# A two-layer RWKV-7 and retention encoder step on one core: full transposes for a pair's states and head factors, branch A's gates left in place, one projection unit moved

## The reference

```python
z = h @ p['w_in']
za, zb, zg = jnp.split(z, [A_COLS, A_COLS + B_COLS], axis=-1)
y_a, new_rwkv = _rwkv7_branch(za_mix, s_rwkv, p)      # 16 heads of 64
y_b, new_ret = _retention_branch(zb, s_ret, pos)      # 4 heads, 256 x 512 states
merged = gates[:, :, 0] * (y_a @ w_branch_a) + gates[:, :, 1] * (y_b @ w_branch_b)
out = merged @ p['w_out']
```

## Time and profile before

| | |
|---|---|
| median of 3 runs | 4438.86 us (4438.25 to 4439.08) |
| the profiled execution | 4447.02 us |
| its span, first to last instruction | 4445.2 us |
| TensorE busy | 4177.0 us, 94% |
| VectorE, ScalarE, GpSimd busy | 44%, 31%, 7% |
| mean granted TensorE clock | 0.964 |
| the eight pairs of layer 0, of layer 1 | 130 to 1188 us, 2360 to 3414 us |
| branch A beside the first head | 1216 to 1327 us, 3441 to 3552 us |

### The profile page before, as it was taken

One profiled execution on the slowest core, in us unless ns is written; L12 is line 12 of the kernel. 1 busy time (PEld: TensorE's weight loads), 2 busy tenths in 40 slices (PEclk: granted clock), 3 DMA queues, 4 the chain that ended last, 5 costly groups with the idle time before them and its releaser, 6 DMA issues.

```text
span 4445.2 us, 86915 instructions
## 1 busy us (share of the span) xinstructions
PE 4177.0 (94%) x37570; PEld 3719.6 (84%) x37570; DVE 1960.5 (44%) x3036; ACT 1389.4 (31%) x2167; POOL 291.5 (7%) x467
## 2 busy tenths in 40 slices
PE   6999999999989988999989999999999899889997
PEld 5888899888866677999978888998888666779997
DVE  3534444434245544333354444444342455454444
ACT  4333333333313223222233233333332132232222
POOL 1000000000011111000100000000000111000000
PEclk8999999999989997999989999999999899989998
DMA  5112212222356564334421122112223565412222
GB/s 186 58 59 66 69 59 62 62 62 70 104 167 207 183 206 150 117 121 125 119 76 59 59 65 68 59 60 64 61 69 109 166 207 181 156 37 74 76 74 69
DMA packets 477367, 448.86 MB, mean 101 GB/s; under 512 B 18894, under 2 KB 409096, under 8 KB 476112
## 3 DMA queue, kind: packets, MB, share of 16 engines
q1 hardware_dynamic: 417712, 253.05, 18.8%
q0 software_dynamic: 41888, 157.01, 10.9%
q10 hardware_dynamic: 17408, 33.56, 2.0%
HBM read 345.79 MB, written 97.76 MB: 100 GB/s over the span
## 4 chain that ended last, share of the span: by engine, by line
PE 85%; DVE 7%; DMA 3%; ACT 3%; issue 2%; POOL 0%; ACTq 0%; DVEq 0%; SPq 0%; POOLq 0%
PE ps L739 83%; DVE scr L1927 2%; PE ps L743 2%; DMA w_raw<-in_w_branch_a_dram 1%; ACT scr L1385 1%; ACT w_hi L1398 1%; DMA scr<-in_ada_w_dram 1%; DVE acc L1927 1%; DVE w_lo L1940 1%; DVE h_lo L1927 1%; DVE lw L1927 1%; DMA w_raw<-in_w_out_dram 1%; DVE scr L1929 0%; ACT scr L1535 0%; DVE acc L2322 0%
## 5 line engine op out<-in xcount | busy, mean ns | idle before, releaser
L739 PE MATMUL ps<-h_hi,w_hi 128*128 128x320 f32 x4544 | 1105.3, 325 | 97.4 <-DVEq L1935 56.1
L739 PE MATMUL ps<-h_lo,w_hi 128*128 128x320 f32 x4544 | 1043.3, 311 | 0.0
L739 PE MATMUL ps<-h_hi,w_lo 128*128 128x320 f32 x4544 | 1041.8, 311 | 0.0
L739 PEld LDWEIGHTS ps<-h_hi,w_hi 128*128 128x128 f32 x4544 | 749.6, 190 | 186.0 <-issue 160.3
L739 PE MATMUL ps<-scr 64*64 64x64 f32 (+10 forms) x13248 | 809.5, 250 | 14.0 <-ACTq L1517 14.0
L739 PEld LDWEIGHTS ps<-scr 64*64 64x64 f32 (+4 forms) x13248 | 590.8, 141 | 212.5 <-issue 182.7
L739 PEld LDWEIGHTS ps<-h_lo,w_hi 128*128 128x128 f32 x4544 | 767.4, 190 | 0.0
L739 PEld LDWEIGHTS ps<-h_hi,w_lo 128*128 128x128 f32 x4544 | 767.0, 190 | 0.0
L1398 ACT ACTIVATE w_hi<-w_raw 128x1024 fp32r<-128x1024 f32 (+1 forms) x468 | 410.7, 878 | 796.5 <-PE ps L739 591.8
L1940 DVE TENSOR_TENSOR w_lo<-w_raw,w_hi 128x1024 fp32r<-128x1024 f32 (+1 forms) x468 | 469.5, 1003 | 366.0 <-ACT w_hi L1398 347.3
L1385 ACT ACTIVATE scr<-ps 128x512 f32<-128x512 f32 (+9 forms) x723 | 343.8, 475 | 759.9 <-PE ps L739 544.4
(11 more groups left out here) (152 smaller groups left out, 2899.7 us busy)
## 6 DMA issues: line engine op xcount, KB each, us to landing
w_raw<-in_w_in_dram SPq DMA_DIRECT2D x180, 512.0 KB, 3.7
scratch_z<-scr SPq DMA_DIRECT2D x128, 320.0 KB, 2.2
scr<-in_ada_w_dram POOLq DMA_DIRECT2D x40, 1024.0 KB, 6.8
scr<-in_state_ret_dram POOLq DMA_DIRECT2D x64, 512.0 KB, 4.9
out_dram<-scr ACTq DMA_DIRECT2D x64, 512.0 KB, 3.0
w_raw<-in_w_ffn_up_dram SPq DMA_DIRECT2D x64, 512.0 KB, 4.0
w_raw<-in_w_ffn_down_dram SPq DMA_DIRECT2D x128, 256.0 KB, 2.7
scr<-scratch_z POOLq DMA_DIRECT2D x24, 1280.0 KB, 9.3
```

Of the source, the lines that this page charges most:

```text
L739: return pe.matmul(out, lhsT, rhs, start=start, stop=stop, skip_group_check=True)
```

## The change

- The sample states of a pair are loaded with the even streams on the first and the odd streams on the last 64 partitions (before: streams 0 to 3 and 4 to 7), so that two streams are turned by one full 128 x 128 transpose: four instead of eight products on the way in (`sT`) and on the way out (`sout`). The stores follow.
- The prompt state is turned in bank 3 instead of bank 4, and the next pair's first scores no longer wait for ScalarE's copy of it; the second block's scores do, with the wait for `sout`.
- `over_channels` becomes five full transposes of factors that VectorE has first widened to 128 x 640 (`widen`), in `yb` for the keys and in `t1` for the group norm.
- The first inverse level: only one of the two orientations of each block is copied through TensorE; the other is multiplied with its mask straight from `LTI` by VectorE, 64 partitions at a time, after the z products.
- `POINTS`: one unit behind the u/w products instead of two, two behind `cb3` instead of one.
- Branch A: the last two gates of a layer are not stored, they stay in `ZT`; the tiles are done in the order 6, 7, 0, ..., 5, so that these two serve first. POOL's two loads go. SyncE's queue issues the weight of a tile first, and then the gate of the tile before.

```diff
@@ -107,6 +107,7 @@
 SPILLED = Z_ALL + 16
+STORED = SPILLED - 2
...
@@ -115,7 +116,7 @@
-POINTS = {"in": 2, "v": 1, "s": 1, "y": 1, "x": 1, "t": 1, "z": 1, "lt": 0, "la": 2, "lb": 2, "uw": 2, "ca": 1, "cb": 1, "pre": 1, "post": 2, "end": 99}
+POINTS = {"in": 2, "v": 1, "s": 1, "y": 1, "x": 1, "t": 1, "z": 1, "lt": 0, "la": 2, "lb": 2, "uw": 1, "ca": 1, "cb": 1, "cb3": 2, "pre": 1, "post": 2, "end": 99}
...
@@ -400,7 +401,6 @@
         stage_sem = {n: sem(n) for n in STAGES}
-        gate_first = [sem("gate_first0"), sem("gate_first1")]
         ya_hi, ya_lo, gate_in = sem("ya_hi"), sem("ya_lo"), [sem("gate_in0"), sem("gate_in1")]
...
@@ -462,7 +462,7 @@
             if name == "ba":
-                return ba_v[l, i]
+                return ba_v[l, (i + KD - 2) % KD]
             if name == "out":
...
@@ -546,18 +546,20 @@
                         sp.wait_ge(lo_done, g - 1)
-                    if name == "ba" and i >= 2:
-                        sp.wait_ge(psum_read_v, freed(g - 1, "v"))
-                        sp.dma_start(ZT[:, i % 2], scratch["z"][GATE0 + i]).then_inc(gate_in[i % 2], 16)
                     sp.dma_start(WR[:, s, 0:kt], weight_of(l, name, i)).then_inc(w_in[s], 16)
+                    if name == "ba":
+                        for t in (i - 1, i) if i == KD - 1 else (i - 1,):
+                            if t >= 2:
+                                sp.wait_ge(psum_read_v, freed(START[l, "ba"] + t - 1, "v"))
+                                sp.dma_start(ZT[:, t % 2], scratch["z"][GATE0 + t - 2]).then_inc(gate_in[t % 2], 16)
                 job_tiles(sp, l, name, tile, 4 if name[0] == "b" else 2)
...
                     for g, kind, i in filler(l, name):
-                        if kind == "own":
-                            spilled[g] = (l * SPILLED + i, i)
+                        if kind == "own" and i < STORED:
+                            spilled[g] = (i, i)
             sp.dma_start(c1[:], io["const1"]).then_inc(const_in, 16)
...
@@ -620,11 +622,11 @@
                         for q in range(2):
-                            po.dma_start(SN[half(e), :, half(q)], io["state_rwkv"][l, 4 * e:4 * e + 4, 2 * p + q].rearrange("b v k -> v b k")).then_inc(rw_in, 16)
+                            po.dma_start(SN[half(e), :, half(q)], io["state_rwkv"][l, e:DEC_B:2, 2 * p + q].rearrange("b v k -> v b k")).then_inc(rw_in, 16)
                     wait_stage(po, "ac_ch", n, "sout")
...
                         for e in range(2):
-                            po.dma_start(outs[6][l, 4 * e:4 * e + 4, 2 * p + q].rearrange("b v k -> v b k"), SN[half(e), :, half(q)]).then_inc(rw_out, 16)
+                            po.dma_start(outs[6][l, e:DEC_B:2, 2 * p + q].rearrange("b v k -> v b k"), SN[half(e), :, half(q)]).then_inc(rw_out, 16)
                         po.dma_start(outs[3][l, 0, 2 * p + q], SPO[0:64, half(q)]).then_inc(rw_out, 16)
...
@@ -656,8 +658,7 @@
                 for i in range(2):
-                    po.wait_ge(z_out[i], 16 * (SPILLED // 2) * (l + 1))
-                    po.dma_start(ZT[:, i], scratch["z"][GATE0 + i]).then_inc(gate_first[i], 16)
+                    po.wait_ge(z_out[i], 16 * (STORED // 2) * (l + 1))
                 wait_stage(po, "ve_gn", PAIRS * l + PAIRS - 1, "ya")
...
@@ -862,8 +863,7 @@
                 for b in range(NBLK):
-                    for q in range(2):
-                        last = mm(five_blocks(5)[half(q), block_of(b)], rows[:, b, q:q + 1].to_broadcast([128, 64]), ident)
+                    last = tr(five_blocks(5)[:, block_of(b)], rows[:, block_of(b)])
                 return last
...
@@ -906,7 +906,7 @@
                 wait_stage(pe, "ve_pr", n, "kr")
-                done(over_channels(KR), "pe_pr", n, "kb")
+                done(over_channels(yb), "pe_pr", n, "kb")
                 yield
...
@@ -927,7 +927,7 @@
                 wait_stage(pe, "ve_gn", n, "gr")
-                done(over_channels(GR), "pe_gn", n, "over")
+                done(over_channels(t1), "pe_gn", n, "over")
                 yield
...
@@ -969,8 +969,8 @@
                         wait_stage(pe, "ve_ch", n - 1, "snew")
+                    elif p:
                         wait_stage(pe, "ac_ch", n - 1, "spo")
-                    elif p:
                         wait_stage(pe, "ac_ch", n - 1, "sout")
...
@@ -989,9 +989,7 @@
                         for d in range(2):
-                            mm(ps[half(d), 2 + g, 128 * (m % 4):128 * (m % 4) + 64], LTI[half(d), m, half(d)], ident[half(d), half(d)])
-                        for d in range(2):
-                            last = mm(ps[half(d), 2 + g, 128 * (m % 4) + 64:128 * (m % 4) + 128], ident[half(d), half(d)], LTI[half(d), m, half(d)])
+                            last = mm(ps[half(d), 2 + g, 64 * (m % 4):64 * (m % 4) + 64], LTI[half(d), m, half(d)], ident[half(d), half(d)])
                     M(last, "pe_in", f"lt{g}")
...
@@ -1072,10 +1070,8 @@
                             wait_stage(pe, "ve_gn", n - 1, "ya")
-                        for b in range(DEC_B):
-                            b = b // 2 + 4 * (b % 2)
-                            e = half(b // 4)
-                            last = mm(ps[:, 5 + b // 4, 64 * (b % 4):64 * (b % 4) + 64], SN[e, b % 4], ident[e, e])
+                        for m in range(DEC_B // 2):
+                            last = tr(ps[:, 5 + m // 2, block_of(m % 2)], SN[:, m])
                         M(last, "pe_ch", "sT")
...
@@ -1104,10 +1100,9 @@
                 W("ve_ch", "snew")
-                M(tr(ps[0:64, 4, 0:128], SS), "pe_ch", "spo")
-                for b in range(DEC_B):
-                    b = b // 2 + 4 * (b % 2)
-                    last = mm(ps[half(b // 4), 2, block_of(b % 4)], TNS[:, b // 2, b % 2], ident)
+                M(tr(ps[0:64, 3, 0:128], SS), "pe_ch", "spo")
+                for m in range(DEC_B // 2):
+                    last = tr(ps[:, 2, block_of(m)], TNS[:, m].rearrange("p e v -> p (e v)"))
                 M(last, "pe_ch", "sout")
...
@@ -1527,7 +1522,7 @@
                         else:
-                            f = l * SPILLED + o
+                            f = l * STORED + o
                             if f >= 2:
...
@@ -1683,7 +1678,7 @@
                     ac.wait_ge(rw_out, 96 * n)
-                do(SPO[0:64, :], ps[0:64, 4, 0:128])
+                do(SPO[0:64, :], ps[0:64, 3, 0:128])
                 M("ac_ch", "spo")
...
@@ -2076,6 +2071,10 @@
+            def widen(out, rows):
+
+                after(ve.tensor_copy(out.rearrange("p (b q n) -> p b q n", b=NBLK, q=2), rows[:, :, :, None].to_broadcast([128, NBLK, 2, 64])))
+
             to_split = []
...
@@ -2110,6 +2109,7 @@
                 after(ve.reciprocal(KR, KR))
+                widen(yb, KR)
                 done("ve_pr", n, "kr")
...
@@ -2161,6 +2161,7 @@
                 after(ve.reciprocal(GR, GR))
+                widen(t1, GR)
                 done("ve_gn", n, "gr")
...
@@ -2212,10 +2213,16 @@
                 for g in range(3):
+                    k = 2 if g == 2 else 4
+                    ms = slice(4 * g, 4 * g + k)
+                    if g == 0:
+
+                        W("pe_in", "z")
+                    for d in range(2):
+                        tt(XX[half(d), ms, 64:128], LTI[half(d), ms, half(d)], c1[half(d), None, C_LC + 64:C_LC + 128].to_broadcast([64, k, 64]), MUL_)
                     W("pe_in", f"lt{g}")
-                    k = 2 if g == 2 else 4
-                    tt(XX[:, 4 * g:4 * g + k], ps[:, 2 + g, 0:128 * k].rearrange("p (t n) -> p t n", n=128),
-                       c1[:, None, C_LC:C_LC + 128].to_broadcast([128, k, 128]), MUL_)
+                    tt(XX[:, ms, 0:64], ps[:, 2 + g, 0:64 * k].rearrange("p (t n) -> p t n", n=64),
+                       c1[:, None, C_LC:C_LC + 64].to_broadcast([128, k, 64]), MUL_)
                     M("ve_in", f"x0.{g}")
...
@@ -2316,10 +2323,10 @@
                             if i < 2:
-                                ve.wait_ge(gate_first[i], 16 * (l + 1))
+                                ve.wait_ge(psum_read_a, freed(START[l, "ba"], "a"))
                             else:
                                 ve.wait_ge(gate_in[i % 2], 16 * ((KD // 2 - 1) * l + i // 2))
-                            ve.tensor_tensor(halves(ACC[:, i]), two_banks(0), halves(ZT[:, i % 2]), MUL_).then_inc(psum_read_v, 1)
+                            ve.tensor_tensor(halves(ACC[:, (i + KD - 2) % KD]), two_banks(0), halves(ZT[:, i % 2]), MUL_).then_inc(psum_read_v, 1)
                         elif name == "bb0":
```

## The result

The changed kernel takes 4377.55 us (median of 4 runs, 4371.16 to 4381.98) against 4438.97 us (4438.25 to 4440.38) beside it: a ratio of 0.9858, 95% interval 0.9846 to 0.9870. In a second series it took 4373.92 against 4442.90, ratio 0.9845 (0.9828 to 0.9862). The forecast was 4367, range 4342 to 4408. The profiled execution fell from 4447.02 to 4371.16 us, its span from 4445.2 to 4369.4.

What follows compares the result with a forecast made beforehand. TensorE, busy 94% of the span, was taken to bound the kernel. Pairs 46 plus branch A 26 made 72 us off the profiled 4447, giving 4375, so 4367 for the median; range 4342 to 4408.

Steps and rivals of the forecast that it cites:

- Branch A, 26 us: Beside the first retention head: weights no longer queue behind gate waits, so TensorE waits less at higher clock; 13 us a layer.
- less one or two for the next wait: Branch A: of 14.4 us a layer, one or two lost to state transfers behind the next head's queries, leaving 13.
- The first inverse level, 15 us: Pairs: half of 80 copying instructions go, VectorE masks six pieces instead; 1.1 us gained a pair, 0.2 lost in pair 0.
- reaches the last group at 687.2: First inverse level: TensorE starts the next level at 686.2, comes to its last group at 687.2; last mask ready at 687.25.
- Head factors, 16.6 us: Pairs: five transposes at 0.65 us replace twenty instructions at 1.24; VectorE's widening hidden except in the first pair's preparation.
- States in and out, 16.3 us: Pairs: four transposes at 0.52 us replace instructions taking about 1.03, gaining 0.51 each way in 16 pairs.
- The bank, 7.8 us: Pair starts: prompt state in bank 3 lets first scores start without ScalarE's copy, freeing 3.9 us of waits a layer.
- The moved unit, -10 us: Chunk 0 of the pairs: eviction falls behind ScalarE's exponentials, waits of 0.8 or 2.1 us; loss of 5.2 us a layer.
- Branch A's wait did not only change its cause: Rival at branch A: the wait only changes its cause and keeps some 22 of 26 us; 4389 us, chance 0.14.
- The rival of a free unit and free masks: Rival in the pairs: moved unit gives +2 instead of -10, first inverse level gives 19 us; 4351 us, chance 0.17.
- the third rival: VectorE and ScalarE take the pairs' gain through dearer pieces and widening; 4396 us, 4408 with half of branch A; chance 0.1.
- the fourth rival: Pairs: clock falls at the new transposes, slowing units behind four groups a pair, 243 us; 4610 us, chance 0.03.

Runs made afterwards that it cites:

- unit_late: Changed kernel with two projection units behind the u/w products, none behind chunk 0's first products and two behind its second: 4357.90 us, ratio 0.9806 to the kernel before.
- states_undone: Changed kernel with sample states in the old stream order, turned by eight multiplies each way: 4384.04 us, ratio 0.9860 to the kernel before.
- factors_undone: Changed kernel with head factors spread by twenty multiplies again, without widening on VectorE: 4396.45 us, ratio 0.9884 to the kernel before.

## Why the prediction held, and where it was off

**The sum.** 72 us were forecast, 46 in the pairs and 26 at branch A; the stages show 39.9 and 29.2, so 69.1. The mechanisms of the terms were right, the sizes partly not, and that 39.9 lies so near to 46 is partly luck: against their terms the level fell 4 us short, the states 8 and the unit 5, while the head factors and what is left for the bank came out 5 us over each. The terms are not independent either, as the bank and the clock show. The forecast median, 4367, was 10.6 us too low in the first series and 6.9 in the second.

**Branch A, 26 us.** Shown as to its cause: the order of one queue is worth 15 us a layer, alone. TensorE's idle time in 111 us is 12.8 us (forecast 11) at a clock of 0.95 (forecast 0.95), and ScalarE has no wait for a weight. The step "less one or two for the next wait" was too careful. That the gates in place save nothing stands too, with the addition that they would have been worth 5 us a layer had the queue been left alone. The rotation's wait reads 8.26 us in the changed kernel instead of 5.70, and yet it stayed as forecast: it ends 20.8 us behind the twelve transposes in both (1236.89 - 1216.07 before, 1212.57 - 1191.76 after). What differs is TensorE's clock on the units ahead of it, 0.50 before and 1.00 after:

```profile
1221.00:1226.00 5.00, 5.00 (x20) 5.00 (x21) 4.53 (x9) 1.73 (x3) 0.00 (x0) 0.50 0.00 0
...
1197.00:1202.00 5.00, 5.00 (x37) 5.00 (x36) 4.51 (x10) 1.43 (x3) 0.00 (x0) 1.00 1.02 377
...
1212.57 0.87 PE L740 MATMUL ps<-r_hi,w_hi 128*128 128x320 f32 x2 [8.26 <-DVE acc L2329]
```

The same kernel run once more (after_again) has 5.69 us in layer 0 and 8.24 in layer 1. TensorE's faster clock ahead of a wait whose end VectorE sets was worth nothing.

**The first inverse level, 15 us.** 11.4 measured, 9.7 without the clock. The step that failed is "reaches the last group at 687.2", against a mask ready at 687.25: equal to within 0.05 us in the prediction, while in the trace of pair 4 the mask comes 0.3 us late, and the same wait of 0.17 us for it stands in every pair but the first, which has 0.8 and 0.4. The prices of the pieces were right to 0.01 us.

**Head factors, 16.6 us.** 21.6 measured in one arrangement and 16.3 in the other; 16.4 without the clock in the first. The row, 0.13 us for a transpose, was exact. The widening (494 ns, forecast 0.55) is hidden in the steady pairs.

**States in and out, 16.3 us.** 8.2 and 11.3 measured; 11.6 without the clock in the first. The length was about right on the way in (0.5 us) but it is worth nothing there, and too small on the way out (0.74 for 0.51). The step that failed is that I took the whole length as gain at a place behind which I had myself written a new eviction wait.

**The bank, 7.8 us.** Not measured alone in the changed kernel. The other terms as undone there (11.4 + 21.6 + 8.2 - 14.6) leave 13 of the 39.9 us for it; on unit_late it is worth 20.3. It was priced by the wait that the kernel before shows, 3.9 us a layer, and should have been priced by the wait that the kernel would have with the shorter way out.

**The moved unit, -10 us.** Its waits are as laid out: 14.9 us in layer 0 for evictions against a forecast of about 15, 2.03 at chunk 0 where a table load is forced, 0.75 in other pairs, 0.46 at chunk 2. Undone it gives back 14.6. The missing step is the clock: a wait of 2 us is sometimes followed by a dip that costs 1.7 or 3.4 us. These dips at chunk 0 cost 6.8 us against 1.7 before. The 5 us more are close to the 6 us by which the pairs fell short of 46, but as the other terms were off both ways, they can't be called their cause alone.

**The rivals.** Branch A's wait did not only change its cause: 29.2 us came off. The rival of a free unit and free masks is out by the same waits. VectorE and ScalarE took part of the pairs' gain, as the third rival had it, but through the order behind each gain and not through dearer pieces. The clock did not fall at the transposes: with 38 of them in a pair the granted clock over layer 0's pairs is 0.99, and unit_late, with all of them in, has 1.00. The Trainium skill, "TensorE: Matmul & The Clock Gate", Part 4, says that transpose mode doesn't count as busy time for the clock as matmuls do; the trace doesn't bear out the fall that the fourth rival took from it, as far as groups of up to nine transposes between matmuls can show. The dips there are stand behind waits, with transposes ahead of them or without: states_undone has sixteen products at that place and two dips.

## What to carry to other kernels

Look in an in-order queue for a load that needs nothing but its buffer and stands behind another that waits: here changing places was worth 30 us, more than any reworked stage. Price a shorter step together with what follows it: half a microsecond saved ahead of a wait is worth nothing, and a cheap step may have been the cover of a copy, so that a part of a change is worth nothing, or more than twice its price, by what else is in it. When the last operand of a batch is forecast to arrive within a tenth of a microsecond of its use, count on its being late, as it was here. And compare where a wait ends before explaining how long it is: the same wait read 5.7 and 8.3 us and ended at the same place.

## What the runs showed of the hardware that was not expected

- **The clock dips behind some short waits.** In the pairs, in stretches otherwise at 1.00, TensorE goes to the lower of its levels at the end of a wait of 1.6 to 2.4 us or up to 1.6 us later, which costs 1.7 us or twice that. It doesn't follow each such wait: of the six equal waits at chunk 0 of pairs 2, 4 and 6 in both layers three were followed by a dip in the changed kernel and all six in factors_undone. There was none at chunk 0 in unit_late, where no wait reaches 1 us. What decides between them stays open.
- **A full float32 transpose is cheap:** five take 0.64 us, where twenty multiplies that spread the same factors took 1.24; on the way out of a pair nine transposes took 1.07 us where five transposes and sixteen instructions of multiplies took 1.81.
- **A second activation table costs little beyond its load:** the exponentials end at 753.35, the load takes 1.28 us from 753.51, and the eviction starts at 754.80, so the change costs 1.45 us in all.
